# Mixing attention values in column tiles, with normalisation and seven of eight query rotations on VectorE

## The reference

```python
    q = (_rmsnorm(q_lat, p["q_norm"]) @ p["w_uq"]).reshape(B, N, N_HEADS, QK_NOPE + QK_ROPE)
    q_nope, q_rope = q[..., :QK_NOPE], q[..., QK_NOPE:]
    ...
        q_rope = _axial_rope(q_rope, tables)
    ...
    def one(qi):
        s = jnp.einsum("bqhd,bkhd->bhqk", qi, k).astype(jnp.float32) * scale
        p = jax.nn.softmax(s, axis=-1).astype(v.dtype)
        return jnp.einsum("bhqk,bkhd->bqhd", p, v)
```

## Time and profile before

| what | value |
| --- | --- |
| median of 3 executions | 2763.88 us (2762.38 to 2764.07) |
| profiled execution | 2761.58 us, span 2759.8 us |
| TensorE busy | 2689.4 us, 97% of the span |
| VectorE busy | 2017.3 us, 73% |
| ScalarE busy | 1216.1 us, 44% |
| GpSimd busy | 622.6 us, 23% |
| granted TensorE clock, mean | 0.994 |
| value mixing (L1107) | 224 records in 16 heads |
| heads of the two mixers | from 599 to 732 us and from 1958 to 2091 us |

### The profile page before, as it was taken

How to read it: one execution, slowest core, us unless ns; L and a number is a source line. 1 busy time by engine, 2 the same in 40 slices (tenths; PEclk the granted TensorE clock), 3 DMA queues, 4 the chain that set the end, 5 groups by cost and what they waited for, 6 DMA issues and landing times. The chain is left out here.

```text
span 2759.8 us, 44748 instructions
## 1 busy us (share of the span) xinstructions
PE 2689.4 (97%) x17878; PEld 2536.0 (92%) x17878; DVE 2017.3 (73%) x2736; ACT 1216.1 (44%) x1998; POOL 622.6 (23%) x323
## 2 busy tenths in 40 slices
PE   6999999999999999999999999999999999999997
PEld 3999999977799999999989999999778999999997
DVE  6878878766534788887888879787664358776876
ACT  5533435556422543343564335355563236443433
POOL 1322422022100124232321413210220002242230
PEclk9999999999999999999999999999999999999999
DMA  6445432210121253423224444322101222212312
GB/s 239 152 147 161 146 123 68 72 56 26 43 84 63 92 168 116 130 99 109 93 101 152 139 159 145 102 75 67 46 27 64 74 65 85 92 63 84 105 49 77
DMA packets 86446, 273.02 MB, mean 99 GB/s; under 512 B 8736, under 2 KB 10016, under 8 KB 86112
## 3 DMA queue, kind: packets, MB, share of 16 engines
q1 hardware_dynamic: 84800, 265.60, 29.1%
q10 hardware_dynamic: 1440, 4.56, 0.5%
HBM read 267.21 MB, written 2.92 MB: 98 GB/s over the span
## 5 line engine op out<-in xcount | busy, mean ns | idle before, releaser
L624 POOL TENSOR_TENSOR sums_raw<-raw_pairs 128x1024 f32<-128x1024 f32 x88 | 238.3, 2708 | 1627.9 <-DVE weights_lo L1706 1050.2
L652 PE MATMUL ps<-h_hi,weights_hi 128*128 128x322 f32 (+1 forms) x1408 | 440.3, 313 | 8.6 <-DVE t_lo L1706 3.1
L656 PE MATMUL ps<-h_hi,weights_lo 128*128 128x322 f32 (+1 forms) x1408 | 437.4, 311 | 0.0
L654 PE MATMUL ps<-h_lo,weights_hi 128*128 128x322 f32 (+1 forms) x1408 | 436.8, 310 | 0.0
L1706 DVE TENSOR_TENSOR weights_lo<-sums_raw,weights_hi 128x1024 fp32r<-128x1024 f32 (+2 forms) x296 | 329.7, 1114 | 56.5 <-ACT weights_hi L1237 26.7
L652 PE MATMUL ps<-t_hi,weights_hi 128*128 128x322 f32 (+1 forms) x1056 | 332.2, 315 | 5.3 <-DVE h_lo L1706 5.3
L652 PE MATMUL ps<-a_hi,weights_hi 128*128 128x320 f32 x1408 | 325.1, 312 | 3.3 <-DVE tmp L1884 2.5
L656 PE MATMUL ps<-t_hi,weights_lo 128*128 128x322 f32 (+1 forms) x1056 | 327.5, 310 | 0.0
L654 PE MATMUL ps<-t_lo,weights_hi 128*128 128x322 f32 (+1 forms) x1056 | 326.4, 309 | 0.0
L654 PE MATMUL ps<-a_lo,weights_hi 128*128 128x320 f32 x1408 | 321.5, 309 | 0.0
L656 PE MATMUL ps<-a_hi,weights_lo 128*128 128x320 f32 x1408 | 321.5, 309 | 0.0
(11 more groups left out here) (273 smaller groups left out, 5680.6 us busy)
## 6 DMA issues: line engine op xcount, KB each, us to landing
raw_pairs<-in_w_up SPq DMA_DIRECT2D x87, 1024.0 KB, 4.9
wm<-in_w_mod SPq DMA_DIRECT2D x88, 512.0 KB, 3.9
raw<-in_w_merge SPq DMA_DIRECT2D x32, 704.0 KB, 4.0
sums_raw<-in_w_down SPq DMA_DIRECT2D x56, 384.0 KB, 3.2
wm<-in_w_mod SPq DMA_DIRECT2D x80, 256.0 KB, 3.0
sums_raw<-in_w_down SPq DMA_DIRECT2D x64, 320.0 KB, 3.0
raw<-in_w_in SPq DMA_DIRECT2D x16, 512.0 KB, 3.6
raw<-in_w_out SPq DMA_DIRECT2D x16, 512.0 KB, 3.5
```

What stands on the lines that cost most here:

```text
L624: nc.gpsimd.tensor_tensor(sums_raw[:, UNIT:3 * UNIT].rearrange("p (s c) -> p s c", s=2), w.rearrange("p (s c) -> p s c", s=2)[:, :, 0:UNIT ...
L652: nc.tensor.matmul(out, whi, v, start=first, stop=False)
L654: nc.tensor.matmul(out, whi, v, start=False, stop=False)
L656: mm = nc.tensor.matmul(out, wlo, v, start=False, stop=last)
```

## The change

1. Value mixing. `values(j)` no longer has ones beside the values. For key tiles 0 to 5 it makes six matmuls: two with the 64 value columns as weights, on query columns 0 to 255 and 256 to 511, into partitions 0 to 63 and 64 to 127 of bank 7, columns 0 to 255; and four with 32 columns of `ones`, on 128 query columns each, into four groups of 32 partitions of bank 7, columns 256 to 383. For key tile 6 it makes two of 64 columns, values and ones, into columns 384 to 511. Banks 1 and 3 are no longer used for it, and `scores(1)` no longer waits for `s_o32`.
2. Normalisation. ScalarE's `o_copy` is gone. VectorE's `o_norm` runs for each head, behind `maximum_lo` of the next: two reciprocals out of PSUM, eight products of 32x128 and one of 64x128, from PSUM to `o32`. It now sets `s_o32`.
3. Rotation. VectorE rotates the queries of heads 1 to 7 of each mixer, as the first thing in its loop; GpSimd keeps head 0.
4. VectorE's two memsets of ones are gone.
5. GpSimd's sums for pair 44 (`pair == 2 * PAIRS`, the first pair of layer 1) wait for one thing more, the last `a_lo` of layer 0.

The diff, without the lines that only follow from these:

```diff
@@ weight_sums (GpSimd) @@
                     pool.wait_ge(s_lo34, pair)
+                    if pair == 2 * PAIRS:
+                        pool.wait_ge(s_alo, pair + START)
@@ the loop of GpSimd @@
-                for h in range(HEADS):
-                    rotate(l * HEADS + h)
+                rotate(l * HEADS)
@@ scores (TensorE) @@
-                    if j == 1:
-                        pe.wait_ge(s_o32, hd)
-                        if h == 0:
-                            pe.wait_ge(s_frlo, (l + 1) * 3)
+                    if j == 1 and h == 0:
+                        pe.wait_ge(s_frlo, (l + 1) * 3)
@@ values (TensorE) @@
-                    out, v_in = (bank(7), ex[j % 2]) if j < 6 else (bank(1 if following else 3, 0, P), ex[j % 2][:, 0:P])
-                    nc.tensor.matmul(out, vals[b][:, j, :], v_in, start=j in (0, 6), stop=j in (5, 6)).then_inc(s_pv, 1)
+                    v = vals[b][:, j, b * VD:(b + 1) * VD]
+                    if j < 6:
+                        for n in range(2):
+                            nc.tensor.matmul(bank(7, 0, S2)[n * VD:(n + 1) * VD], v, ex[j % 2][:, n * S2:(n + 1) * S2],
+                                             start=j == 0, stop=False)
+                        for n in range(4):
+                            mm = nc.tensor.matmul(bank(7, S2, S2 + P)[32 * n:32 * n + 32], ones[:, 0:32],
+                                                  ex[j % 2][:, n * P:(n + 1) * P], start=False, stop=j == 5)
+                    else:
+                        nc.tensor.matmul(bank(7, S2 + P, S2 + 2 * P)[0:VD], v, ex[j % 2][:, 0:P], start=True, stop=True)
+                        mm = nc.tensor.matmul(bank(7, S2 + P, S2 + 2 * P)[VD:P], ones[:, 0:VD], ex[j % 2][:, 0:P],
+                                              start=True, stop=True)
+                    mm.then_inc(s_pv, 1)
@@ attend (ScalarE) @@
-                if h == HEADS - 2:
-                    maximum_copy(hd + 1)
-                o_copy(hd)
-                if h < HEADS - 2:
                     maximum_copy(hd + 1)
@@ mixer_step (VectorE) @@
-                for s in range(2):
-                    c = (1 - s) * VD
-                    nc.vector.memset(vals[s][:, :, c:c + VD], 1.0)
...
                 for h in range(HEADS):
-                    if h and h % 2 == 0:
-                        o_norm(l, h // 2 - 1)
+                    if h + 1 < HEADS:
+                        rotate(hd0 + h + 1)
                     weight_lo(c0 + HEADS_C + h + 2)
...
                         maximum_lo(hd0 + h + 1)
-                o_norm(l, OT - 1)
+                    o_norm(hd0 + h)
@@ o_norm (VectorE) @@
+            def o_norm(hd):
+                rows0 = hd % 2 * VD
+                dve.wait_ge(s_pv, (hd + 1) * 7)
+                nc.vector.reciprocal(sums_inv[:, 0:P], bank(7, S2, S2 + P))
+                nc.vector.reciprocal(sums_inv[VD:P, P:2 * P], bank(7, S2 + P, S2 + 2 * P)[VD:P]).then_inc(s_rinv, 1)
+                dve.wait_ge(s_rinv, hd + 1)
+                for n in range(4):
+                    for r in range(0, VD, 32):
+                        tt(o32[rows0 + r:rows0 + r + 32, TOK[n]:TOK[n] + P],
+                           bank(7, n % 2 * P, (n % 2 + 1) * P)[n // 2 * VD + r:n // 2 * VD + r + 32],
+                           sums_inv[32 * n:32 * n + 32, 0:P], ALU.mult)
+                tt(pro(o32[rows0:rows0 + VD]), bank(7, S2 + P, S2 + 2 * P)[0:VD], sums_inv[VD:P, P:2 * P],
+                   ALU.mult).then_inc(s_o32, 1)
```

More of the change, by code:

```diff
@@ L344, in build @@
         vt = tmp[:, 2 * SAMPLE + 2 * T:2 * SAMPLE + 2 * T + KEYS]
-        sums = acc
+        sums_inv = acc[:, 0:2 * P]
         mod_acc = [tmp[:, g * D:(g + 1) * D] for g in range(2)]
@@ L440, in build @@
         s_st, s_exp, s_pv = sem("scores_ready"), sem("exp_ready"), sem("values_mixed")
-        s_o32, s_rinv, s_on = sem("o_copied"), sem("row_inverse"), sem("o_normed")
+        s_o32, s_rinv = sem("o_normed"), sem("row_inverse")
         s_ohi, s_olo = sem("o_hi_ready"), sem("o_ready")
@@ L1582, in maximum_copy @@
                 nc.scalar.activation(q_hi[hd % 2][QK:QK + 2, :], ps[0:2, 5 * 512:5 * 512 + T], ACT.Copy).then_inc(s_rowc, 1)
-            def o_copy(hd):
-                s = hd % 2
-                o_rows, s_rows = slice(s * VD, (s + 1) * VD), slice((1 - s) * VD, (2 - s) * VD)
-                act.wait_ge(s_pv, (hd + 1) * 7)
-                act.wait_ge(s_olo, hd // 2)
-                for dst, rows in ((o32, o_rows), (sums, s_rows)):
-                    nc.scalar.activation(two(dst[o_rows]), bank(7)[rows].rearrange("p (a n) -> p a n", a=2), ACT.Copy)
-                    ins = nc.scalar.activation(pro(dst[o_rows]), bank(1 if (hd + 1) % HEADS else 3, 0, P)[rows], ACT.Copy)
-                ins.then_inc(s_o32, 1)
             def o_hi(l, t):
-                act.wait_ge(s_on, l * OT + t + 1)
+                act.wait_ge(s_o32, (l * OT + t + 1) * 2)
                 nc.scalar.activation(ot_hi[:, t, :], o32[:], ACT.Copy).then_inc(s_ohi, 1)
```

16 lines of the change are left out of this document (8 added, 8 removed).

## The result

The changed kernel takes 2810.39 us (median of 4 runs, 2808.48 to 2810.98); the kernel before took 2763.98 in runs beside it (4 runs, 2762.38 to 2764.36). The ratio is 1.0168, 95% interval 1.0150 to 1.0185: slower by 46.4 us. The forecast was 2787.5 with a range up to 2804. Its direction and its main mechanism hold, its size does not: it had half of the loss.

The account below looks back on a forecast made before the run. TensorE was taken to bound the kernel. Mixing +26.3, last-head handover +0.9, memsets -1.6 and GpSimd's sums -1.8 gave +23.8 us on 2761.58; with 2.3 for the median, 2787.5 us was forecast, range 2766 to 2804.

Parts of the forecast that it names:

- main mechanism: In value mixing, TensorE drains at switches of tiling mode, outweighing saved streaming: +0.28 us per key tile, +26.3 us for 16 heads.

Follow-up runs that it names:

- e15: Changed kernel with GpSimd rotating the queries of all heads again; 2808.62 us, ratio 1.0163 to the kernel before.
- e8: Changed kernel with the values too in tiles of 32 columns, four passes in place of two of 64; 2778.58 us, ratio 1.0052.
- e3: Changed kernel with VectorE's eight normalising products on 32 partitions replaced by seven on 128, results not normalised; 2793.63 us, ratio 1.0107.
- e11: Kernel before with eight unread products filling TensorE's wait in the Fourier stage; 2762.95 us, ratio 0.9996.
- e4: Kernel before with some 5.4 us of unread VectorE additions that the last head's first value product waits for; 2773.35 us, ratio 1.0033.
- e5: Kernel before with VectorE rotating the queries of heads 1 to 7, placed ahead of the normalisation; 2789.18 us, ratio 1.0080.
- e6: Kernel before with only GpSimd's added wait ahead of the sums for pair 44; 2763.76 us, ratio 0.9998.
- e1: Changed kernel with the last head of a mixer mixing its values into bank 2 instead of bank 7; 2789.22 us, ratio 1.0091.
- e9: Changed kernel with values in tiles of 32 and bank 2 for the last head of a mixer; 2773.14 us, ratio 1.0034.
- e12: e9 with key tiles mixed in three visits instead of six, and ScalarE splitting the merge's weights one exponent later; 2757.16 us, ratio 0.9974.
- e13: e12 with eight unread products filling TensorE's wait in the Fourier stage; 2755.64 us, ratio 0.9970.
- e2: Changed kernel with nine unread products in TensorE's wait ahead of the last head's mixing; 2790.69 us, ratio 1.0098.

## What to carry over

A wait of the busiest engine is not priced by its length: look at the granted clock behind it, first where nothing else can fill the stretch, and if the wait can't be removed, give TensorE unread products to do in it. When a matmul is packed in column tiles, count visits to the tiled mode, not only columns (0.33 us each here), keep one tile width within a visit, and group the work of several tiles into one. A queue's order matters even on an engine with time to spare: ask what stands behind a moved step, and who waits for that.

## What the runs showed of the hardware

- **The granted clock after idle time.** In the last heads it fell behind waits of 0.78 and 1.95 us (changed kernel, e15; e8 with 1.98) in six of six, behind 0.78 and 1.05 in one of two (e3), behind 0.78 and 0.58 in one of two in e11, in the second mixer of e4, and in none of six in the kernel before, e5 and e6, and behind 0.78 alone in none of eight (e1, e9, e12, e13). With unread products in the longer wait it didn't fall (e2). Other waits of about 2 us, in the Fourier stage, in the first mixer of e4 and in e5, lowered it often but not always. The Trainium skill ("TensorE: Matmul & The Clock Gate", Part 1) has idleness lower the clock and activity release it; the rows agree with the first.
- **How long it stays down.** With the last head mixed in tiles of 64 and 32 it lasted into the merge, 17 to 20 us, in all five cases (changed kernel, e15, once in e3). With tiles of 32 only it lasted 3.4 us (e8, two of two), with whole-array mixing about 7 (e4, two of two), though TensorE's records fill the time behind the wait in all of them. Why the lengths differ wasn't tried, and stays open.
- **VectorE's overlap of neighbours.** Products of 128 columns out of PSUM that follow each other without a wait start 0.20 us apart on 128 partitions, all operands from partition 0 (e3), and 0.30 apart on 32 partitions with start partitions that change (changed kernel), each 0.28 long in the records. An instruction on 64 partitions from partition 0 does overlap with its follower (1.00 us to the next start for 1.08 of its own, kernel before), so the number of partitions alone is not the reason.
- **The change of tile shape** costs 0.34 us for entering and leaving (e12 against e8), and 0.15 between two tile widths (changed kernel against e8). The row maxima, a tile of two columns, cost only 0.05.
